# The first modulation in column quarters, each followed by its part of three contraction chunks

## The reference, cut to what matters

```python
mod = silu(c) @ w_ada + b_ada            # 2048 -> 6 * 2048: shift_m, scale_m, gate_m, shift_f, scale_f, gate_f
h = rmsnorm(x, g_norm_mix) * (1 + scale_m) + shift_m
proj = h @ w_in                          # 256 x 2048 @ 2048 x 3904
# proj is cut into dq, dk, dv (differential attention, 8 heads), q_lat, kv_lat, k_pe (latent attention, 8 heads)
q, kv = rmsnorm(q_lat) @ w_q_b, rmsnorm(kv_lat) @ w_kv_b
x = x + gate_m * (concat(o_diff, o_mla) @ w_out)
```

## Time and profile before

| | us |
|---|---|
| median of 3 runs | 2731.72 |
| profiled execution, whole | 2736.53 |
| its span | 2734.8 |
| TensorE busy | 2591.3 (95%) |
| VectorE busy | 1637.2 (60%) |
| ScalarE busy | 1212.2 (44%) |

### The profile page before, as it was taken

How to read it: one execution, slowest core, us unless ns; L and a number is a source line. 1 busy time by engine, 2 the same in 40 slices (tenths; PEclk the granted TensorE clock), 3 DMA queues, 4 the chain that set the end, 5 groups by cost and what they waited for, 6 DMA issues and landing times.

```text
span 2734.8 us, 30664 instructions
## 1 busy us (share of the span) xinstructions
PE 2591.3 (95%) x11981; PEld 2147.4 (79%) x11981; DVE 1637.2 (60%) x1806; ACT 1212.2 (44%) x1630; POOL 10.8 (0%) x62
## 2 busy tenths in 40 slices
PE   1599879799999999999999999999999999999999
PEld 1477767688888888888888888888888888888887
DVE  6889687577554555556555675556555554455554
ACT  1345544444433444444444665454444344344443
POOL 0000000000000000000000000000000000000000
PEclk9999999899999999999999999999999999999999
DMA  9898558477655556555554584445555555555554
GB/s 382 304 346 319 179 201 295 177 261 278 225 188 197 185 186 200 197 185 185 185 185 157 162 270 140 137 143 190 177 185 184 199 186 198 188 187 196 187 197 139
DMA packets 254815, 566.08 MB, mean 207 GB/s; under 512 B 9967, under 2 KB 25068, under 8 KB 242156
## 3 DMA queue, kind: packets, MB, share of 16 engines
q1 hardware_dynamic: 252164, 562.87, 60.1%
q10 hardware_dynamic: 2538, 1.65, 0.2%
HBM read 562.39 MB, written 2.10 MB: 206 GB/s over the span
## 4 chain that ended last, share of the span: by engine, by line
PE 87%; DVE 7%; DMA 4%; issue 1%; ACT 1%; ACTq 0%; DVEq 0%
PE acc L470 80%; DVE acc_ada L1545 3%; PE tp L494 3%; DMA w_raw<-in_w_ada_dram 2%; DVE w_lo L429 2%; DMA w_raw<-in_w_in_dram 1%; PE sc L2977 1%; ACT w_hi L424 0%; PE sc L3069 0%; PE sc L3068 0%; PE sc L3085 0%; PE sc L2605 0%; PE tp L2700 0%; DMA rowsA<-in_g_norm_mix_dram 0%; PE tp L2790 0%
## 5 line engine op out<-in xcount | busy, mean ns | idle before, releaser
L429 DVE TENSOR_TENSOR w_lo<-w_raw,w_hi 128x1024 fp32r<-128x1024 f32 (+2 forms) x878 | 1053.4, 1217 | 582.3 <-ACT w_hi L424 574.2
L424 ACT ACTIVATE w_hi<-w_raw 128x1024 fp32r<-128x1024 f32 (+2 forms) x878 | 912.4, 1054 | 875.4 <-PE acc L470 783.7
L470 PE MATMUL acc<-w_hi,h_hi 128*128 128x512 f32 (+2 forms) x2272 | 713.9, 395 | 8.8 <-DVE h_lo L1630 4.4
L470 PE MATMUL acc<-w_lo,h_hi 128*128 128x512 f32 (+2 forms) x2272 | 700.6, 390 | 0.0
L470 PE MATMUL acc<-w_hi,h_lo 128*128 128x512 f32 (+2 forms) x2272 | 699.5, 389 | 0.0
L470 PEld LDWEIGHTS acc<-w_lo,h_hi 128*128 128x128 f32 x2272 | 428.0, 189 | 88.9
L470 PEld LDWEIGHTS acc<-w_hi,h_lo 128*128 128x128 f32 x2272 | 428.1, 189 | 88.6
L470 PEld LDWEIGHTS acc<-w_hi,h_hi 128*128 128x128 f32 x2272 | 417.6, 189 | 92.7 <-issue 7.2
L470 PE MATMUL acc<-w_hi,f_hi 128*128 128x512 f32 x864 | 268.7, 392 | 0.0
L470 PE MATMUL acc<-w_hi,f_lo 128*128 128x512 f32 x864 | 266.1, 389 | 0.0
L470 PE MATMUL acc<-w_lo,f_hi 128*128 128x512 f32 x864 | 266.0, 389 | 0.0
(11 more groups left out here) (423 smaller groups left out, 1686.6 us busy)
## 6 DMA issues: line engine op xcount, KB each, us to landing
w_raw<-in_w_ff_dram SPq DMA_DIRECT2D x128, 1024.0 KB, 5.2
w_raw<-in_w_in_dram SPq DMA_DIRECT2D x108, 1024.0 KB, 4.9
w_raw<-in_w_ada_dram SPq DMA_DIRECT2D x96, 1024.0 KB, 6.7
w_raw<-in_w_ffn_gate_dram SPq DMA_DIRECT2D x44, 1024.0 KB, 5.0
w_raw<-in_w_ffn_up_dram SPq DMA_DIRECT2D x44, 1024.0 KB, 5.0
w_raw<-in_w_ffn_down_dram SPq DMA_DIRECT2D x44, 1024.0 KB, 5.0
w_raw<-in_w_out_dram SPq DMA_DIRECT2D x32, 1024.0 KB, 5.1
w_raw<-in_w_up_fox_dram SPq DMA_DIRECT2D x8, 1024.0 KB, 5.0
```

The source lines that it names most:

```text
L424: nc.scalar.activation(dst, src, ACT.Copy).then_inc(hi_done, 1)
L429: nc.vector.tensor_tensor(dst, src, hi.bitcast(F32), ALU.subtract).then_inc(lo_done, 1)
L470: last = nc.tensor.matmul(acc[b][:, t, 0:width], st[:, kt, t * P:(t + 1) * P], w[:, slot, kt - 2 * j, 0:width], start=(kt == 0 and n == 0) ...
```

## The change

The first 32 macs of 128x2048 are replaced by 64 steps on 128 x (2 x 512): a *quarter* is 512 columns of shift and the same 512 of scale, through all 16 row tiles. The loads of w_ada for them hold four row tiles of 512 columns (2 KB rows), and a step of four row tiles (`front_macs`) takes one load of shift and one of scale. When a quarter is finished, its four row tiles of h can be made, and with them the matching four row tiles of w_in's column chunks 0, 1 and 2 are multiplied (24 halves in all, 6 per quarter), chunk 2 in the two banks `sc`. `FRONT` is the order of the loads. The input x is loaded ahead of all. ScalarE makes all of xs and h_hi, VectorE h_lo. Of the macs of chunks 0 to 2, 10 are moved behind: two more in chunk 6, two more in chunk 7, two more in the latent attention's loop and four more in the output projection. The first four heads begin six steps later, the rotary parts 0 and 1 stand at steps 26 and 28 in place of 16 and 22, and `gate_sum` is behind the attention's loop.

```diff
-FIRST_MACS = ((0, 2), (0, 1, 2, 3), (0, 1, 2, 3), (0, 1, 2, 3), (0, 1, 2, 3), (0, 1, 2, 3), (0, 2), (1,)) + 7 * ((0,),)
+FIRST_MACS = ((), (), (), (0, 1, 2, 3), (0, 1, 2, 3), (0, 1, 2, 3), (0, 1, 2, 3), (0, 1, 3)) + 7 * ((0,),)
 FIRST_TILES = {"w_in": KD, "w_q_b": 4, "w_kv_b": 2}
-HEAD_AT = (30, 33, 36, 39, 53, 56, 59, 62)
+FRONT_CHUNKS, QUARTERS = 3, 4
+FRONT = (("ada", 0, 0), ("ada", 0, 1), ("ada", 0, 2), ("ada", 0, 3),
...
+HEAD_AT = (36, 39, 42, 45, 53, 56, 59, 62)
...
+        mix_acc = place("mix_acc", [P, QUARTERS, 2, CW], F32, 0)
...
+        front_load, at = {}, 0
+        for what in FRONT:
+            assert what[0] == "w" or at % 2 == 0
+            front_load[what] = at
+            at += 2 if what[0] == "ada" else 1
+        def front_half(q, nth):
+            return 2 * (FRONT_CHUNKS * q + nth)
+        first_half, first_load, first_mac, half = {}, {}, {}, 2 * FRONT_CHUNKS * QUARTERS
...
-            ada_loads(RING)
             sp.dma_start(x[:], A["x"][0].rearrange("(t p) d -> p t d", p=P)).then_inc(S("x_loaded"), 16)
-            ada_loads(2 * KD - RING)
-            for nth in range(len(FIRST)):
-                if nth == 1:
+            for (kind, q, k), L in front_load.items():
+                if kind == "ada":
+                    for g in range(2):
+                        at = g * D + q * CW
+                        src = A["w_ada"][0][CW * k:CW * (k + 1), at:at + CW].rearrange("(k p) n -> p k n", p=P)
+                        ring(At(L + g), raw[:, At(L + g).slot(RING)], src, mac_done, At(2 * (4 * q + k + 1)))
+                else:
+                    name, col, width, nk = first_part(k)
+                    src = A[name][0][CW * q:CW * (q + 1), col:col + width].rearrange("(k p) n -> p k n", p=P)
+                    ring(At(L), raw[:, At(L).slot(RING)], src, lo_done, At(front_half(q, k) + 2))
+            macs_so_far = 2 * KD
...
-            ada_loads(HEADS)
-            weights(A["w_out"][0], 4, KD, macs=2)
+            ada_loads(HEADS + 2)
+            weights(A["w_out"][0], 4, KD, macs=3, uniform=0)
...
+            act.wait_ge(S("mix_var"), 1)
+            nc.scalar.activation(stat[:, 4:6], stat[:, 2:4], ACT.Sqrt).then_inc(S("mix_std"), 1)
+            act.wait_ge(S("mix_rstd"), 1)
+            for c in range(4):
+                cols = slice(c * CW, (c + 1) * CW)
+                for t in range(NT):
+                    nc.scalar.activation(xs[:, t, cols], x[:, t, cols], ACT.Copy, scale=stat[:, 6 + t:7 + t]).then_inc(
+                        S(f"mix_xs{t}"), 1)
+            def front_hi(q, nth):
+                name, col, width, nk = first_part(nth)
+                for jj in range(2):
+                    h, L = At(front_half(q, nth) + jj), At(front_load["w", q, nth])
+                    hi, lo, src = half_places(h, L, jj, 2, width)
+                    split_hi(act, h, L, jj, hi, src)
+            def front_piece(p):
+                q, u = p // 2, At(2 + 3 * (p // 2) + p % 2)
+                act.wait_ge(S("mod_made"), q + 1)
+                bank, free = tp_wait(act, u)
+                if p >= 2:
+                    act.wait_ge(S("mix_ready"), p - 1)
+                for kk in range(2):
+                    k = 2 * p + kk
+                    link(nc.scalar.activation(ttmp[p % 2][:, kk, :], bank[:, kk * T:(kk + 1) * T], ACT.Identity,
+                                              scale=gmod[:, k:k + 1], bias=modT[:, k:k + 1]))
+                nc.scalar.activation(h_hi[:, 2 * p:2 * p + 2, :], ttmp[p % 2][:], ACT.Copy).then_inc(free, 1)
+            for q in range(QUARTERS):
+                if q % 2 == 0:
+                    front_hi(q, 0)
+                front_hi(q, 1)
+                front_piece(2 * q)
+                front_piece(2 * q + 1)
+                front_hi(q, 2)
+                if q % 2 == 0:
+                    front_hi(q + 1, 0)
+            use = 14
...
-            macs(20)
-            bank, free = tp_wait(dve, At(1))
-            V.tensor_copy(vecB[:, 0:NROWS], bank[:, 0:NROWS]).then_inc(free, 1)
-            macs(2)
-            norm("mix")
-            macs(1)
-            scaled("mix", range(2, 4))
-            macs(1)
-            mod_column(0, 2)
-            macs(2 * KD - macs_so_far)
...
+            def front_macs(q, quad, ks=range(4)):
+                L, to = At(front_load["ada", q, quad]), mix_acc[:, q]
+                r = L.slot(RING)
+                for kk in ks:
+                    k = 4 * quad + kk
+                    w = raw[:, r:r + 2, kk, :]
+                    if kk == 0:
+                        for g in range(2):
+                            dve.wait_ge(raw_loaded[r + g], L.round(RING).times(16).val(16))
+                    if k == 0:
+                        last = V.tensor_scalar(to, w, cT[:, 0:1], None, ALU.mult)
+                    else:
+                        if kk == 0:
+                            dve.wait_ge(S("mac_done"), 2 * (4 * q + quad))
+                        last = V.scalar_tensor_tensor(to, w, cT[:, k:k + 1], to, ALU.mult, ALU.add)
+                    if kk < 3:
+                        link(last)
+                    else:
+                        last.then_inc(S("mac_done"), 2)
...
+            def front_mods(q):
+                bank, free = tp_wait(dve, At(1 + 3 * q))
+                ks, to = slice(4 * q, 4 * q + 4), slice(KD + 4 * q, KD + 4 * q + 4)
+                V.tensor_tensor(modT[:, ks], bank[:, 0:4], vecA[:, ks], ALU.add)
+                link(V.tensor_tensor(modT[:, to], bank[:, 4:8], vecA[:, to], ALU.add))
+                dve.sem_inc(free, 1)
+                link(V.scalar_tensor_tensor(gmod[:, ks], modT[:, to], 1.0, vecA[:, 112 + 4 * q:116 + 4 * q], ALU.add, ALU.mult))
+            def front_piece(p):
+                u = At(2 + 3 * (p // 2) + p % 2)
+                dve.wait_ge(tp_free[u.slot(2)], u.round(2).val(1))
+                ks = slice(2 * p, 2 * p + 2)
+                V.tensor_tensor(h_lo[:, ks, :], ttmp[p % 2][:], h_hi[:, ks, :].bitcast(F32), ALU.subtract).then_inc(
+                    S("mix_ready"), 1)
...
+            def mix_statistics():
+                dve.wait_ge(S("mix_sumsq"), 4)
+                token_sums(stat[:, 0:2], 0)
+                V.tensor_scalar(stat[:, 2:4], stat[:, 0:2], 1.0 / D, EPS, ALU.mult, ALU.add).then_inc(S("mix_var"), 1)
+                dve.wait_ge(S("mix_std"), 1)
+                link(V.reciprocal(stat[:, 6:8], stat[:, 4:6]))
+                dve.sem_inc(S("mix_rstd"), 1)
+            front_macs(0, 0)
+            mix_statistics()
+            for quad in range(1, 4):
+                front_macs(0, quad)
+            for q in range(QUARTERS):
+                if q % 2 == 0:
+                    front_lo(q, 0)
+                    front_lo(q, 1)
+                    front_mods(q)
+                    front_macs(q + 1, 0, range(3))
+                    front_piece(2 * q)
+                    front_piece(2 * q + 1)
+                    front_macs(q + 1, 0, range(3, 4))
+                    front_macs(q + 1, 1)
+                    front_lo(q, 2)
+                    front_lo(q + 1, 0)
+                    front_macs(q + 1, 2)
+                    front_macs(q + 1, 3)
+                else:
+                    if q < QUARTERS - 1:
+                        front_macs(q + 1, 0)
+                        front_mods(q)
+                        front_lo(q, 1)
+                    else:
+                        front_lo(q, 1)
+                        front_mods(q)
+                    front_piece(2 * q)
+                    front_piece(2 * q + 1)
+                    front_lo(q, 2)
+                    if q < QUARTERS - 1:
+                        for quad in range(1, 4):
+                            front_macs(q + 1, quad)
+            macs_so_far = 2 * KD
+            positions()
+            angles(0)
+            angles(1)
+            dve.sem_inc(S("angles_reduced"), 1)
+            lambdas(3)
+            bank, free = tp_wait(dve, At(13))
+            link(V.tensor_copy(vecB[:, 0:NROWS], bank[:, 0:NROWS]))
+            dve.sem_inc(free, 1)
+            use = 14
...
-                    one_mac()
+                one_mac()
...
+            def front_sums(q):
+                u = At(1 + 3 * q)
+                b = u.slot(2)
+                if q:
+                    pe.wait_ge(tp_free[b], u.round(2).val())
+                pe.wait_ge(S("mac_done"), 8 * (q + 1))
+                for k in range(8):
+                    last = MM(tp[b][:, k:k + 1], mix_acc[:, q, k // 4, k % 4 * P:(k % 4 + 1) * P], ones[:, 0:1],
+                              start=True, stop=True)
+                last.then_inc(tp_full[b], 1)
+            for q in range(QUARTERS):
+                front_sums(q)
+                for t in range(NT):
+                    pe.wait_ge(S(f"mix_xs{t}"), q + 1)
+                for k in range(2):
+                    TR(pe, At(2 + 3 * q + k), grid(xs, q * CW + 2 * k * P))
+                for nth in range(FRONT_CHUNKS):
```

(16 more changed lines are left out.)

265 lines of the change are left out of this document (112 added, 153 removed).

## The result

| | before | after |
|---|---|---|
| median, us | 2732.35 (4 runs) | 2759.05 (4 runs, 2754.71 to 2761.14) |
| profiled execution, us | 2736.53 | 2754.71 (span 2752.8) |
| ratio | 1 | 1.0088, 95% interval 1.0074 to 1.0103 |

By the ratio the change makes the kernel 24 us slower (20 to 28).

The account below looks back on a forecast made before the run. The first 100 us were taken as set by w_ada loads and VectorE's macs, not TensorE. Front 11.1 plus 5.6 behind gave +16.7 us, a median of 2748.4; range 2738 to 2758, for 8 of 10 2720 to 2770.

Parts of the forecast that it names:

- the sum: Whole kernel: front 11.1 us plus 5.6 us behind it, +16.7 us; given 0.45 for 2738 to 2754.
- The new steps: VectorE's smaller macs in the front: 1.28 us each, 1.37 us with the wait between them.
- The start: VectorE waits for ScalarE's squares of x behind its first group: list ends at 21.6 us, VectorE let go at 28.8.
- The price of the loads: w_ada loads of the front with 2 KB rows: 3.11 us each, with 2.73 as the other end.
- The walk: Four queues followed through the front: quarters of 40 us, half 24 at 192.4 us, front loses 11.1 us.
- rival (c): TensorE runs the front's halves at half clock after pauses: 2781 if all 24 do; 0.10 with other slow mixes.
- Behind half 24: Moved macs, rotary parts and gate sums behind the front: +5.6 us, with bounds 0 and +20.
- Rival (a): Front: the overlap works, VectorE waits for nothing from 28.8 us to its last w_lo; 2719 us, chance 0.17.
- Rival (b): Start: ScalarE's DMA list stays slow, +8.1 us on all quarters, 2756 us; chance 0.18.
- Rival (d): Whole kernel: no matter, with fast loads, cheap steps (front 0) and macs hidden; 2731 to 2737 us, chance 0.10.

Follow-up runs that it names:

- before_2kb: The kernel before, with its first 32 w_ada loads taken as 512 x 512 blocks with 2 KB rows (modulation computed from wrong elements); ratio to before 1.0011.
- warm: The kernel after, with 28 extra unused matmuls on TensorE ahead of its wait for the macs of quarters 1, 2 and 3; ratio to before 1.0097.
- fine_slots: The kernel after, with w_ada slots given back half a group earlier, by twice as many DMAs of half the size; ratio to before 1.0054.
- fine_all: The kernel after, with slots returned half a group earlier, statistics behind the third group of macs, and gains transposed early; ratio to before 1.0012.

## Why the prediction held, step by step

The direction and its main reason held: the steps with their waits set the pace, the quarters came 38 us apart (38 to 41 forecast), and the front lost 12.5 us for 11.1. The close match of the sum (16.7 us forecast, 18.2 in the profiled executions) is partly luck. Terms of both signs were wrong, and the match is with the fastest of four executions: by the ratio the loss is 24 us, and the median of 2759.05 us is 11 us above the forecast of 2748 and just outside the 2738 to 2758 given for the sum. It lies within 2720 to 2770.

**The new steps** (1.28 us, 1.37 apart) measured 1.284 and 1.34. Right.

**The start.** ScalarE's list ended sooner than before, but its squares began at 24.56 us, not 21.6, and the small steps behind them took longer than counted. Four issues of 0.96 to 1.33 us stand in the middle of the list; the two long ones of the earlier trace rows are gone. The statistics let VectorE go on at 32.3 us, not 28.8, where before they had no hold on it. The wait was named right: but for three small instructions VectorE stood still from 20.4 to 32.3 us, 12 us for the 9.5 of the forecast. Taken away, it is worth 6 to 7 us of the front, by two kernels. The steps of quarter 0 ended at 50.4 us for 48.3.

**The price of the loads** is the term that was wrong: 3.11 us, taken from a stream with pauses. In a steady stream they take 2.55 us. A pair arrives 6.96 us after its issue, where I had 8.1. Less two times 2.55 that leaves 1.9 us, the latency that I had; but mine came from 5.0 - 3.11, so this agreement is by chance (5.0 - 2.55 would be 2.45). The error lay in the method: bytes and DMA share give 3.11 us per load in rows 7, 2.89 in the quarters of the kernel after and 2.71 in before_2kb, so a price by the share came out higher where the stream had pauses. The Trainium skill (DMA: Bandwidth & Descriptors, Specifications) has 512 B as the least size for full rate; the measurement agrees with it for 2 KB (2.55 us a load for 2.73 with rows of 8 KB), and I had let the wrong row decide.

**The walk** gave quarters of 40 us; they are 38.3. The waits are of its kinds but mostly smaller: 0.6 to 2.6 us for w_ada (2.8 forecast), at most 1.6 for just-in-time loads (2.9), 4.95 and 1.47 in the odd quarters (5.6). The end of quarter 3 came 3 us before the forecast, at 165.5 for 168.5, though quarter 0 had ended 2 us behind it. That this is due to the cheaper loads is argued from the pair's 6.96 us; no kernel changed their price alone in this front.

**TensorE's clock** took that back. The walk had nothing for it; rival (c) counted 1.3 to 2.6 us per quarter. At the end it costs more, since there nothing hides it: the sums of quarter 3 take 3.55 us (1.95 in warm), and the last six halves 13.77 + 5.44 = 19.2 us, not the 16.4 of the walk. The window over it:

```profile
172.00:180.00 8.00, 7.26 (x21) 5.75 (x21) 1.96 (x3) 2.67 (x4) 0.00 (x0) 0.61 0.38 145
```

A granted clock of 0.61 is a mix of the 1.2 and 2.4 GHz levels, behind a pause of 7.74 us. From the end of the steps to half 24 the walk had 23.9 us; it took 28.2. So the front's 11.1 us came out as 12.5 by misses of opposite sign: some 2 us more at the start, 5 less in the three quarters, 4 more behind them.

**Behind half 24** I had +5.6, and it is +6.0 in the profiled execution, again from other terms. By the drains and chains of the two kernels: -4.9 up to chunk 6's drain (294.12 to 301.75 us), of which 3.7 is the sum that moved on, so the rest is 1.2 us shorter where I had +3.9, and neither the mac of chunk 6 nor the rotary part shows; +5.0 in chunk 7, 3.6 of it that sum; +3.0 in the queries and latents (0 forecast, and its cause isn't shown); -1.7 in the attention's loop, which fits the 1.72 us of gate sums in the earlier trace rows; +3.2 at its end for these sums and +1.4 for the projection's first halves at half clock, where I had +1.7 for these three together. The error there was to price the sums as work: they also stand ahead of ScalarE's w_hi (0.6 us each in its queue) and leave TensorE a pause of 2.98 us.

**Rival (a)**, a quarter under 34.5 us, would have needed what fine_slots does, and even that gave 35.3 to 36.2. Its objection, that the slots come back late whatever the rates, is what the runs bear out. **Rival (b)** came by less than half: the two long issues went, and VectorE was let go at 32.3 us, between the 28.8 of the sum and the 36.9 of the rival. **Rival (c)** came in part, as above. **Rival (d)** failed by the start's pause alone.

What stays open: why the kernel after takes 2754.5 to 2765.0 us from run to run. Its two profiled executions differ by 10.2 us. Half 24 starts only 0.5 us apart; 1.9 us come from there to the drain of chunk 6, 2.7 in chunk 7, 1.1 up to the output projection, and 3.8 behind its end, most of them near 1690 us, in the stretch that fine_all's traces showed. The mean clock between 300 and 345 us is 0.96 and 0.89:

```profile
300.00:345.00 45.00, 36.98 (x228) 32.40 (x226) 32.29 (x59) 26.09 (x65) 0.00 (x0) 0.96 0.57 202
```

```profile
300.00:345.00 45.00, 41.44 (x239) 36.26 (x238) 29.45 (x51) 23.63 (x62) 0.00 (x0) 0.89 0.56 200
```

The clock goes with it; what tips it was not tried. This is also why a sum of terms from one pair of traces can't be held to a few microseconds here.

## What to carry to other kernels

Work brought forward into an idle engine is worth nothing while what feeds it sets the pace: here VectorE and the ring of four slots do, and TensorE's 42 us of idle time at the start were free anyway. With a short ring, look first at when a slot is given back and not at how fast it is filled: halving the unit of return, at the same bytes and work, was worth 9 us. The price of a load is read from a stream that never pauses. A step that is taken over to a place where nothing waited (here the statistics) should be put where its input is surely there, and a gain ahead should be followed to the end of the stage, since 6 to 7 us of it were lost again behind.

## What the runs showed of the hardware

Loads of 1.049 MB with rows of 2 KB ran at 2.55 us each in before_2kb, faster than those with rows of 8 KB (2.73 us in rows 6), on the same engines and in the same stretch. By the bytes moved it was 2.57 us up to 46 us and 2.59 behind, against 2.66 and 2.79.

Next to SyncE's loads with rows of 2 KB, ScalarE's issue of w2v took 0.49 us (before_2kb) and 0.69 us (after), where it took 4.07 next to rows of 8 KB. But issues in the middle of the same list took up to 1.33 us in after, and why isn't shown.

Matmuls put into a pause did not keep the clock up for the work behind it where other pauses followed: in quarter 1 of warm pauses of 2.01, 2.69 and 2.25 us came between the filler and the first half, and that half took 5.07 us, where a half takes 2.73 us at full clock.

The same code took 3.1 us more or less at one place near 1680 us, with TensorE busy throughout, as the granted clock over 20 us was 0.66 or 0.83.
